# Two query products side by side before a phase boundary, and two weight chunks loaded and split ahead of it

## What is computed

```
x  = x + g1 * (mixed @ w_out)
h2 = rmsnorm(x, norm2_g) * (1 + sc2) + sh2
q  = (h2 @ w_query)                     # 16 halves of 128: 8 heads x 2
scores = einsum('thpd,hpnd->thpn', q, sub_keys)
s_top, i_top = top_k(scores, 16)        # then pairs, experts, gates
x  = x + g2 * peer(h2, ...)
# beside it, per sample sequence and head, the new delta state (an output):
S = S * exp(gl) + k_tail^T v_new
```

## Time and profile before

| | |
|---|---|
| median of 3 runs | 2006.64 us (2002.65, 2007.5, 2006.64) |
| the profiled execution | 2003.99 us, its span 2002.1 us |
| TensorE busy | 1906.5 us, 95% |
| VectorE busy | 1547.6 us, 77% |
| ScalarE busy | 843.2 us, 42% |
| GpSimd busy | 744.2 us, 37% |
| mean granted TensorE clock | 0.986 of full |

### The profile page before, as it was taken

One profiled execution on the slowest core, in us unless ns is written; L12 is line 12 of the kernel. 1 busy time (PEld: TensorE's weight loads), 2 busy tenths in 40 slices (PEclk: granted clock), 3 DMA queues, 4 the chain that ended last, 5 costly groups with the idle time before them and its releaser, 6 DMA issues.

```text
span 2002.1 us, 33599 instructions
## 1 busy us (share of the span) xinstructions
PE 1906.5 (95%) x12681; PEld 1711.4 (85%) x12681; DVE 1547.6 (77%) x2994; ACT 843.2 (42%) x1449; POOL 744.2 (37%) x575
## 2 busy tenths in 40 slices
PE   5989999999999998888989999999999999999997
PEld 3679999999976898887888889988998898889886
DVE  4466666676665788999966788888888887988787
ACT  3333443334333234599973333333333333333333
POOL 0010000000025333789952444444444555545462
PEclk8999999999999998899999999999999999999999
DMA  8812222222271324566778999999999999999974
GB/s 355 321 60 80 70 73 76 70 70 65 69 286 64 134 68 138 191 193 189 201 238 309 366 365 344 348 351 343 333 356 349 342 340 352 346 343 344 352 271 147
DMA packets 173246, 466.05 MB, mean 233 GB/s; under 512 B 16032, under 2 KB 72704, under 8 KB 169760
## 3 DMA queue, kind: packets, MB, share of 16 engines
q1 hardware_dynamic: 127008, 296.13, 42.1%
q0 software_dynamic: 46080, 167.79, 22.7%
HBM read 422.24 MB, written 41.62 MB: 232 GB/s over the span
## 4 chain that ended last, share of the span: by engine, by line
PE 49%; DVE 11%; POOL 2%; issue 2%; DMA 2%; ACT 2%; DVEq 0%; SPq 0%; ACTq 0%
PE pp L2534 20%; PE dd L2547 17%; PE pp L2547 8%; POOL hot_a L2318 2%; PE dd L2502 2%; PE pp L2174 1%; DMA v_raw<-in_v 1%; DVE top_i L2217 1%; DVE top_i L2206 1%; DVE less L2207 1%; DVE top L2748 1%; DVE top_v L2201 1%; DVE top_v L2212 1%; DVE hot_b L2770 1%; DVE cand L2858 1%
## 5 line engine op out<-in xcount | busy, mean ns | idle before, releaser
L426 ACT ACTIVATE w_hi<-w_raw 128x1024 fp32r<-128x1024 f32 x204 | 214.9, 1053 | 172.0 <-PE pp L442 116.3
L2534 PE MATMUL pp<-act_hi,w_hi 128*128 128x384 f32 x792 | 268.6, 339 | 1.7 <-DVE acc L3005 1.7
L2534 PE MATMUL pp<-act_lo,w_hi 128*128 128x384 f32 x792 | 266.9, 337 | 0.0
L2534 PE MATMUL pp<-act_hi,w_lo 128*128 128x384 f32 x792 | 266.2, 336 | 0.0
L442 PE MATMUL pp<-act_hi,w_hi 128*128 128x272 f32 x1056 | 243.1, 312 | 7.4 <-DVE act_lo L747 4.4
L430 DVE TENSOR_TENSOR w_lo<-w_raw,w_hi 128x1024 fp32r<-128x1024 f32 x177 | 219.4, 1239 | 33.3 <-ACT w_hi L426 33.3
L442 PE MATMUL pp<-act_lo,w_hi 128*128 128x272 f32 x1056 | 218.8, 289 | 0.0
L442 PE MATMUL pp<-act_hi,w_lo 128*128 128x272 f32 x1056 | 218.8, 289 | 0.0
L2701 ACT ACTIVATE co_hi<-cf 128x384 fp32r<-128x384 f32 x128 | 67.5, 528 | 347.9 <-PE pp L2547 302.5
L442 PEld LDWEIGHTS pp<-act_hi,w_hi 128*128 128x128 f32 x1056 | 164.9, 190 | 25.6 <-issue 17.6
L2997 DVE TENSOR_TENSOR v_lo<-v_raw,v_hi 128x1024 fp32r<-128x1024 f32 x128 | 156.6, 1223 | 36.7 <-ACT v_hi L2703 34.8
(11 more groups left out here) (433 smaller groups left out, 4450.1 us busy)
## 6 DMA issues: line engine op xcount, KB each, us to landing
w_raw<-in_stream SPq DMA_DIRECT2D x206, 512.0 KB
v_raw<-in_v SPq DMA_DIRECT2D x128, 512.0 KB
ada_w<-in_ada SPq DMA_DIRECT2D x24, 1024.0 KB, 11.6
gt<-gate_matrix SPq DMA_DIRECT2D x31, 768.0 KB
gate_matrix<-gstage SPq DMA_DIRECT2D x11, 2048.0 KB, 9.7
early<-cst SPq DMA_DIRECT2D x28, 192.0 KB, 4.1
cst<-early SPq DMA_DIRECT2D x28, 192.0 KB
wrow<-in_wout SPq DMA_DIRECT2D x8, 512.0 KB, 7.4
```

The costliest lines, as they stand in the source:

```text
L426: nc.scalar.activation(w_hi[k.slot][:], w_raw[k.slot][:], ACT.Copy).then_inc(w_hi_done, 1)
L2534: last = nc.tensor.matmul(pp[s][:, 0, 0:TD], w[:, c * P:(c + 1) * P], a[:, c, 0:TD], start=(c == 0 and w is w_hi[s] and a is act_hi), stop ...
```

## The change

It has three parts.

**Loads and splits moved ahead.** SyncE loads query chunk 3 in the third block, behind chunk 2 and ahead of the sub-keys. At the end of the third block ScalarE makes the high parts and VectorE the low parts of chunks 2 and 3; both vanish from the fourth block. In the fourth block SyncE loads chunks 4 and 5 first, and the pairs of state stores follow behind the loads of chunks 5, 6, 7 and 8.

**Products of chunks 0 and 1 side by side.** For every feature chunk and column half TensorE does the three matmuls of chunk 0 and then the three of chunk 1, in two PSUM banks. The product of chunk 1 leaves the fourth block, and the half products of 2 and 3 move up one place each between the states; all of chunk 3 now stands ahead of score 0.

**One decay moved ahead.** GpSimd decays head 1 in the third block, once seven feature chunks of `act_lo` are ready; its wait for the low part of chunk 3 in the fourth block goes.

```
 # third block, GpSimd, at its end
+                pool.wait_ge(h2_lo_done, KC - 1)
+                state_decayed(pool, 1)
 # third block, SyncE
-                for k in range(3):
+                for k in range(4):
                     load_chunk(sp, Chunk(C_QUERY + k))
 # third block, TensorE
+                pe.wait_ge(strips_read, 2)
+                def first_queries(b, c):
                     pe.wait_ge(h2_lo_done, c + 1)
+                    for i in range(2):
+                        for w, a in ((q_hi[i], act_hi), (q_hi[i], act_lo), (q_lo[i], act_hi)):
+                            last = nc.tensor.matmul(pp[Chunk(C_QUERY + i).slot][:, b, 0:HN], w[:, c * P:(c + 1) * P],
+                                                    a[:, c, b * HN:(b + 1) * HN], ...)
 # third block, ScalarE, behind high2(7)
+                for i in range(2, 4):
+                    k = Chunk(C_QUERY + i)
+                    act.wait_ge(w_landed[k.slot], 16 * k.turn + 16)
+                    nc.scalar.activation(w_hi[k.slot][:], w_raw[k.slot][:], ACT.Copy).then_inc(w_hi_done, 1)
 # third block, VectorE, behind low2(7)
+                for i in range(2, 4):
+                    split_lo(dve, Chunk(C_QUERY + i))
 # fourth block, GpSimd
-                for h in range(1, H):
+                for h in range(2, H):
                     state_decayed(pool, h)
-                pool.wait_ge(w_lo_done, Chunk(C_QUERY + 4).n)
 # fourth block, SyncE
-                for k in range(2, 2 * H + 4):
-                    if k > 2:
-                        load_chunk(sp, Chunk(C_QUERY + k))
-                    if k - 2 < H // 2:
-                        sp.wait_ge(new_added, 2 * (k - 2) + 2)
+                for k in range(4, 2 * H + 4):
+                    load_chunk(sp, Chunk(C_QUERY + k))
+                    if 0 <= k - 5 < H // 2:
+                        sp.wait_ge(new_added, 2 * (k - 5) + 2)
 # fourth block, TensorE
-                product(pe, Chunk(C_QUERY + 1), w_hi=q_hi, w_lo=q_lo)
+                product(pe, Chunk(C_QUERY + 2), first)
                 for m in (2, 3):
                     new_state(pe, m)
-                product(pe, Chunk(C_QUERY + 2), first)
+                product(pe, Chunk(C_QUERY + 2), second)
                 for m in (4, 5):
                     new_state(pe, m)
-                product(pe, Chunk(C_QUERY + 2), second)
+                product(pe, Chunk(C_QUERY + 3), first)
                 for m in (6, 7):
                     new_state(pe, m)
-                product(pe, Chunk(C_QUERY + 3), first)
+                product(pe, Chunk(C_QUERY + 3), second)
                 pe.wait_ge(keys_ld, 16)
                 pe.wait_ge(new_added, KC)
                 score(0)
                 score(1)
-                product(pe, Chunk(C_QUERY + 3), second)
                 score(2)
 # fourth block, ScalarE
-                    split_hi(act, c + 2)
+                    if k >= 2:
+                        split_hi(act, c + 2)
 # fourth block, VectorE
-                split_lo(dve, Chunk(C_QUERY + 2))
                 for m in range(KC):
                     state_added(dve, m)
-                    if m == 2:
-                        split_lo(dve, Chunk(C_QUERY + 3))
```

More of the change, by code:

```diff
@@ L431, in split_lo, with product @@
                                     ALU.subtract).then_inc(w_lo_done, 1)
-        def product(pe, k, part=range(KC), w_hi=w_hi, w_lo=w_lo):
+        def product(pe, k, part=range(KC)):
             s = k.slot
@@ L1868, in _ @@
                 last.then_inc(folded, 1)
[L1870 to L1874, removed]
-                    pe.wait_ge(h2_lo_done, c + 1)
[L1877 to L1882, removed]
+                for i in range(2):
+                    k = Chunk(C_QUERY + i)
+                    pe.wait_ge(w_lo_done, k.n + 1)
+                    pe.wait_ge(pp_read[k.slot], k.turn + 1)
@@ new lines, in _ @@
+                pe.wait_ge(strips_read, 2)
+                def first_queries(b, c):
+                    pe.wait_ge(h2_lo_done, c + 1)
+                    for i in range(2):
+                        for w, a in ((q_hi[i], act_hi), (q_hi[i], act_lo), (q_lo[i], act_hi)):
+                            last = nc.tensor.matmul(pp[Chunk(C_QUERY + i).slot][:, b, 0:HN], w[:, c * P:(c + 1) * P],
+                                                    a[:, c, b * HN:(b + 1) * HN],
+                                                    start=(c == 0 and w is q_hi[i] and a is act_hi),
+                                                    stop=(c == KC - 1 and w is q_lo[i]))
+                        if b == 1 and c == KC - 1:
+                            last.then_inc(pp_done[Chunk(C_QUERY + i).slot], 1)
@@ L1884, in _ @@
                 for c in range(3):
-                    first_query(0, c)
+                    first_queries(0, c)
                 pe.wait_ge(sq_own_done, 1)
                 nc.tensor.matmul(b_ss_s, ones, sq_own[:], start=True, stop=True).then_inc(ss_s_done, 1)
-                first_query(0, 3)
+                first_queries(0, 3)
                 pe.wait_ge(rt_s_done, 1)
                 new_state(pe, 1)
-                first_query(0, 4)
+                first_queries(0, 4)
                 pe.wait_ge(h2_lo_s, 1)
@@ L1893, in _ @@
                 for c in range(5):
-                    first_query(1, c)
+                    first_queries(1, c)
                 for c in range(5, KC):
                     for b in range(2):
-                        last = first_query(b, c)
-                last.then_inc(pp_done[k.slot], 1)
+                        first_queries(b, c)
             @block.scalar
@@ L2328, in _ @@
             def _(sp):
-                for k in range(2, 2 * H + 4):
-                    if k > 2:
-                        load_chunk(sp, Chunk(C_QUERY + k))
-                    if k - 2 < H // 2:
-                        sp.wait_ge(new_added, 2 * (k - 2) + 2)
-                        for h in range(2 * (k - 2), 2 * (k - 2) + 2):
+                for k in range(4, 2 * H + 4):
+                    load_chunk(sp, Chunk(C_QUERY + k))
+                    if 0 <= k - 5 < H // 2:
+                        sp.wait_ge(new_added, 2 * (k - 5) + 2)
+                        for h in range(2 * (k - 5), 2 * (k - 5) + 2):
                             sp.dma_start(delta_s_out[h], s_s[:, h]).then_inc(out_st, 16)
```

## The result

| | before | after |
|---|---|---|
| median | 2007.5 us (2002.65 to 2012.04, 9 runs) | 2000.06 us (1994.93 to 2003.45, 9 runs) |
| profiled execution: span | 2002.1 us | 1998.7 us |

The ratio is 0.9959, with a 95% interval from 0.9947 to 0.9971: faster by 0.41%, 8.2 us of 2007.5. The prediction was 1996.1 us with 1991.5 to 2001.5, from a gain of 9.2 us.

What follows compares the result with a forecast made beforehand. Bound: chunk 3's late load and split ahead of the state products, then selections in step with TensorE's products. 7.6 us up to score 0 plus 1.6 from slack ahead of chunk 4: 2005.3 - 9.2 = 1996.1 us, range 1991.5 to 2001.5.

Steps and rivals of the forecast that it cites:

- The chain through chunk 3's load: Boundary into fourth block: chunk 3's load, its split and queued state additions leave TensorE idle 4.85 us; that goes.
- The third block: After the samples' wait, 66 matmuls at full clock, 0.129 us each, 8.5 us, end at 639.6.
- Rival (a): Third block: clock falls at 629 all the same, 2.2 us later; gain 7.0 us, 1998.3 us; chance 15%.
- rival (d): Third block's tail: clock stays low throughout, 6.9 us later; gain 2.3 us, 2003.0 us; chance 12% with other small losses.
- The other engines at the boundary: End of third block: ScalarE done at 635.2, VectorE's splits about 638, hidden behind TensorE's end at 639.6.
- the upper bound: End of third block: `low2` held for a decay, both splits 2.75 us, VectorE ends 641.3, boundary 1.7 us later.
- To score 0: Fourth block: start 640.8, four half products of 3.1, three state pairs of 1.9, score 0 at 658.9, 7.6 us earlier.
- From score 0 to product 4: Behind score 0: TensorE waits for chunk 4's low part, product 4 starts 664.5, 9.2 us earlier than 673.72.
- The selections: VectorE behind score 0: copies held by GpSimd's low parts, selections keep step with products, 9.2 us earlier.
- Rival (b): Selections keep their own start, since a copy is not held: gain 7.6 us, 1997.7 us; chance 7%.
- Rival (c): Behind score 0: low clock costs 3.3 us, VectorE slips past one low part; gain 13.3, 1992.0 us; chance 12%.
- Rival (e): Fourth block: GpSimd's decays become the bound, score 0 at 660.7; slower than before 4%, at 2008 us or more.

Runs made afterwards that it cites:

- the first part alone: Against the kernel before: chunk 3 loaded, chunks 2 and 3 split, head 1 decayed ahead of the boundary, product 1 still behind it; ratio 0.9966, again 0.9972.
- the second part alone: Against the kernel before: chunks 0 and 1 side by side, new order of half products, loads, splits and decays unmoved; ratio 1.0015, again 1.0008.
- two kernels with free copies: Changed kernel with both copies behind a selection written as maxima over a length-one axis, ratio 0.9944; also with chunk 3's last quarter behind score 1, 0.9943.

## Why the prediction was right

**What bounded the kernel.** The chain through chunk 3's load was read rightly: the first part alone removed it, brought product 4 forward by 6.8 us and gave 0.9966. But the prediction took the whole 4.85 us for the price of the load's place in the queue. The second profile of the kernel before shows that 1.55 of them were the split held by the last decay, which does not happen in every execution.

**The third block.** Forecast: 66 matmuls from 631.11, end at 639.6. Measured 643.18 - 3.50 = 639.68. The clock was the choice here and full clock was right, in both profiles of the changed kernel. Rival (a), low clock at the same place, and rival (d), low clock over the whole tail, did not come. (Their prices were a little off: 25 and 72 matmuls at 0.101 us more each are 2.5 and 7.3 us and not 2.2 and 6.9, less what the wait for the samples hides.)

**The other engines at the boundary.** Forecast "about 638" for VectorE; measured 641.40 - 3.50 = 637.90. The two pieces were off in opposite ways: `low2` was held until the decay ended, as in the upper bound, and the splits, which came behind the decay, were not held at all. TensorE came last, as said.

**To score 0.** Forecast 658.9, measured 662.80 - 3.50 = 659.30. The term that was too small is the half product: I took half of 6.18, 3.1 us, and 647.54 less 644.37 is 3.17; the four together took 12.68 and not 12.4, the three pairs of states 5.75 and not 5.7. The first product started at 640.87 (forecast 640.8).

**From score 0 to product 4.** Forecast 664.5, measured 668.26 - 3.50 = 664.76, that is 8.96 us earlier and not 9.2. TensorE waited for chunk 4's low part, as worked out. The kernel with chunk 3's last quarter moved took away 1.05 of the 1.15 us of waits between score 0 and product 4.

**The selections.** Copy 1 fell inside GpSimd's low part and left with it, so VectorE followed TensorE. Rival (b), selections that keep their own start, is out: the second copy ends 72.71 us behind the mark, before the change 81.67, so it moved by the 8.96 us of product 4 and not by the 7.2 of score 0. In all ten profiles with the copies left as they were, the copy behind the third selection takes 1.46 to 1.49 us. Rival (c), a missed low part, did not happen; it needed a low clock behind score 0, and the clock was full to the end of the selections. Rival (e) is out by the additions and by the decay put back, which cost 0.46 us. The profile puts one wait of VectorE, ahead of the additions at 653.90, down to GpSimd, but that pair starts 1.24 us behind the start of its state product like the two pairs at 648.78 and 659.02, the decays it needs had been done for 2 us (six take 1.88 us each from 644.41), and TensorE waited for no addition.

**The size.** 8.96 us at product 4 against 8.2 us in the ratio, inside its interval (5.8 to 10.6 us). That the two agree so well is in part luck. The profile that I worked from has the later product 4 of the two, 1.55 us of it by that hold: against the second profile of the kernel before, the gain there is 6.75 us, and the same working from that profile would have forecast about 7.0 (9.2 less 2.2, an estimate), while the two timings gave 8.2 and 9.2. And behind the selections some comes and goes. The stretches behind them, before and after:
```profile
900.00:910.00 10.00, 7.89 (x57) 7.47 (x57) 8.82 (x48) 8.57 (x21) 6.99 (x7) 1.00 0.17 62
```
```profile
900.00:910.00 10.00, 8.47 (x51) 8.51 (x52) 8.66 (x45) 8.54 (x24) 6.34 (x6) 0.83 0.38 113
```
The clock drops there in the changed kernel's profile and not in the first of the kernel before. But the second profile of the kernel before has such a drop too:
```profile
904.00:914.00 10.00, 7.89 (x47) 7.60 (x46) 9.27 (x46) 8.45 (x20) 7.41 (x7) 0.83 0.25 71
```
so the new order is not needed for it. The first product of the last stage stands 435.38 and 432.8 us behind the mark in the two profiles of the kernel before, and 428.35 and 428.37 in those of the changed kernel: 4.4 to 7.0 us earlier, against 6.75 to 8.96 at product 4. The change gives back about 2 us on that way.

The profiles tell where. At the first gather of expert rows nothing is lost yet: 197.81 and 195.57 us behind the mark before, 188.23 and 188.26 after. From there to the last stage there are two forms, which go with the copy behind the last selection. In five profiles it takes 0.20 or 0.22 us, as before the change, and the way is 237.2 to 237.8 us long. In six it meets GpSimd's low part and takes 1.73 to 1.76 us, and the way is 239.8 to 240.3 us long:
```profile
780.77 1.75 DVE L2754 COPY top<-top_v 128x64 f32<-128x64 f32 x1 [0.24 <-DVE top_i L2228]
```
Both profiles of the kernel before are of the first form; both of the changed kernel, both of the second part alone and the one with the decay put back are of the second; the first part alone has one of each. So the changed kernel ran in the longer form, 2.5 to 2.9 us more, and the prediction, which followed the selections only to their second copy, had no term for it. Why the way behind the gather is longer is not shown. (The two kernels with free copies lie between, at 238.5.) The 8.2 and 9.2 us of the two timings are more than the 4.4 to 7.0 left at the last stage, but their intervals reach down to 5.8 and 6.4; what of the rest is chance I can't say from two profiles each.

**The absolute time.** The forecast of 1996.1 is 4.0 us under the measured 2000.06. Of this 2.2 us are the start: I took 2005.3 us for the kernel before, and with nine runs its median is 2007.5. The rest is the gain, 7.4 us between medians and not 9.2.

## What to carry to other kernels

A load that stands on its queue behind a store's wait can hold up engines that never touch the store: follow the queue order back from the idle engine, and look for other work queued behind the late split. Work moved to the near side of a phase boundary pays only if what it used to cover moves with it; the side-by-side products alone cost what they gave. Where two engines end an instruction within 0.1 us of each other again and again, as here, test whether one paces the other, and relieve every instruction that could take the waiting one's place. And a wait read from one profile can hold a chance meeting (here 1.55 of 4.85 us): a second profile of the unchanged kernel shows it, if both are read from a mark just ahead of the change.

## What the runs showed of the hardware

A copy and a conversion on VectorE, 0.20 and 0.18 us when alone, were held for 1.3 us by an elementwise GpSimd instruction, whichever of the two met it; a maximum over an axis of length one, with the same data, took 0.22 us inside the same GpSimd instruction. The Trainium skill, page "SBUF — State Buffer", section "Who interferes with whom", names copy and cast among the operations that can take the port pair shared with GpSimd, and says that `tensor_reduce` never contends on trn2; the traces agree on all three.

Instructions with two inputs in SBUF met GpSimd's decays in the same way, and the one that started later was held: VectorE's `low2`, 0.75 us alone, took 2.35 when it started 0.12 us behind a decay; its split of a chunk, 1.23 alone, took 2.78 when it started 0.20 us behind one; and a decay, 1.91 alone, took 2.91 when it started 0.08 us behind the split.

Where the two products ran side by side, the granted clock stayed at full (2.4 GHz) through the tail of the third block. Both profiles of the kernel before and both of the first part alone, in which chunk 0 is multiplied alone, have a low stretch there (the first of the latter is shown, mean 0.52 over 10 us); none of the nine profiles with the products side by side has one (1.00 from 22 to 38 us behind the mark). The first part alone differs from the changed kernel only in the products, so their order is the cause. The side-by-side order both fills the wait of 0.93 us and adds matmuls to the thin stretch, and which of the two keeps the clock is not shown.
```profile
627.00:637.00 10.00, 9.71 (x37) 7.50 (x37) 9.56 (x17) 5.70 (x10) 1.47 (x1) 0.52 0.01 2
```
